# Second attention: the scores from two products with k's high and low parts in one tile, and the rope of k finished on VectorE

## What is computed

```python
q1 = _apply_rope(qp[0], cos, sin); q2 = _apply_rope(qp[1], cos, sin)
...
def block(i):                                     # 128 queries at a time
    qpos = start + jnp.arange(Q_BLOCK)
    mask = kpos[None, :] < ((qpos // CHUNK) + 1)[:, None] * CHUNK
    s1 = jnp.einsum('bhqd,bhkd->bhqk', qb1, k1).astype(jnp.float32) * scale
    s2 = jnp.einsum('bhqd,bhkd->bhqk', qb2, k2).astype(jnp.float32) * scale
    p1 = jax.nn.softmax(jnp.where(mask, s1, -jnp.inf), axis=-1)
    p2 = jax.nn.softmax(jnp.where(mask, s2, -jnp.inf), axis=-1)
    a = (p1 - lam * p2).astype(v.dtype)
    return jnp.einsum('bhqk,bhkd->bhqd', a, v)
```

## Time and profile before

| | |
|---|---|
| median of 3 runs | 1842.66 us (1841.44 to 1843.53) |
| the profiled execution: its own time | 1840.62 us |
| its span, first to last instruction | 1838.8 us |
| PE busy | 1800.9 us, 98% of the span |
| VectorE, ScalarE, GpSimd busy | 733.5, 780.1, 1021.7 us (40%, 42%, 56%) |
| share of PE in the chain that ended last | 90% |
| mean granted clock of PE | 0.994 of full speed |

### The profile page before, as it was taken

One profiled execution on the slowest core, in us unless ns is written; L12 is line 12 of the kernel. 1 busy time (PEld: TensorE's weight loads), 2 busy tenths in 40 slices (PEclk: granted clock), 3 DMA queues, 4 the chain that ended last, 5 costly groups with the idle time before them and its releaser, 6 DMA issues.

```text
span 1838.8 us, 27037 instructions
## 1 busy us (share of the span) xinstructions
PE 1800.9 (98%) x8880; PEld 1500.3 (82%) x8880; DVE 733.5 (40%) x1348; ACT 780.1 (42%) x1612; POOL 1021.7 (56%) x919
## 2 busy tenths in 40 slices
PE   8999999999999999999999999989999999999997
PEld 6879888888887888888888888878887888888886
DVE  7954000001135555453333322456765543333224
ACT  5434323222244555464444422545564644444221
POOL 6856655555462322366666655556554566666651
PEclk9999999999999999999999999999999999999999
DMA  5312333323334544223333233333332233332332
GB/s 150 92 29 86 104 99 95 91 85 105 89 100 100 129 119 114 81 81 103 103 91 103 78 105 91 83 81 86 86 82 56 81 103 95 99 94 86 103 90 96
DMA packets 327250, 171.92 MB, mean 93 GB/s; under 512 B 43458, under 2 KB 316948, under 8 KB 327188
## 3 DMA queue, kind: packets, MB, share of 16 engines
q1 hardware_dynamic: 327172, 171.12, 33.4%
q10 hardware_dynamic: 16, 0.00, 0.0%
HBM read 152.15 MB, written 2.10 MB: 84 GB/s over the span
## 4 chain that ended last, share of the span: by engine, by line
PE 90%; DVE 4%; ACT 2%; POOL 1%; issue 1%; DMA 1%; SPq 0%; DVEq 0%; ACTq 0%; POOLq 0%
PE bank L920 25%; PE bank L921 24%; PE bank L922 24%; PE attended L920 2%; PE attended L922 2%; PE attended L921 2%; PE turned L1317 1%; PE bank L1023 1%; PE bank L1011 1%; PE score L1299 1%; DVE xres L2001 1%; PE score L1301 0%; ACT xres L1510 0%; PE score L1300 0%; DVE small L2271 0%
## 5 line engine op out<-in xcount | busy, mean ns | idle before, releaser
L703 POOL TENSOR_TENSOR WL<-raw,WH 128x512 fp32r<-128x512 f32 (+3 forms) x656 | 776.4, 1206 | 615.2 <-ACT WH L1474 614.5
L920 PE MATMUL bank<-XL,WH 128*128 128x512 f32 x1456 | 579.3, 398 | 7.2 <-DVE XL L2044 3.6
L921 PE MATMUL bank<-XH,WH 128*128 128x512 f32 x1456 | 567.3, 390 | 0.0
L922 PE MATMUL bank<-XH,WL 128*128 128x512 f32 x1456 | 567.1, 389 | 0.0
L1474 ACT ACTIVATE WH<-raw 128x512 fp32r<-128x512 f32 (+3 forms) x656 | 338.3, 565 | 303.9 <-PE bank L922 201.5
L920 PEld LDWEIGHTS bank<-XL,WH 128*128 128x128 f32 x1456 | 274.5, 189 | 62.8 <-DVE XL L2044 4.8
L922 PEld LDWEIGHTS bank<-XH,WL 128*128 128x128 f32 x1456 | 274.4, 188 | 57.8
L921 PEld LDWEIGHTS bank<-XH,WH 128*128 128x128 f32 x1456 | 274.9, 189 | 51.2
L920 PE MATMUL bank<-HL,WH 128*128 128x512 f32 (+1 forms) x528 | 200.5, 380 | 0.0
L921 PE MATMUL bank<-HH,WH 128*128 128x512 f32 (+1 forms) x528 | 200.3, 379 | 0.0
L922 PE MATMUL bank<-HH,WL 128*128 128x512 f32 (+1 forms) x528 | 200.2, 379 | 0.0
(11 more groups left out here) (314 smaller groups left out, 2492.7 us busy)
## 6 DMA issues: line engine op xcount, KB each, us to landing
raw<-in_ffn_w_in SPq DMA_DIRECT2D x88, 512.0 KB, 3.8
raw<-in_w_gate SPq DMA_DIRECT2D x22, 512.0 KB, 3.8
raw<-in_w_up SPq DMA_DIRECT2D x22, 512.0 KB, 3.9
raw<-in_ffn_w_out SPq DMA_DIRECT2D x28, 384.0 KB, 3.4
raw<-in_ffn_w_out SPq DMA_DIRECT2D x28, 320.0 KB, 3.1
raw<-in_a_w_in SPq DMA_DIRECT2D x16, 512.0 KB, 4.1
raw<-in_kv_w SPq DMA_DIRECT2D x32, 256.0 KB, 3.2
raw<-in_w_in SPq DMA_DIRECT2D x12, 512.0 KB, 3.9
```

Source lines behind the costliest of these rows:

```text
L703: pool.tensor_tensor(wl, x, wh, ALU.subtract).then_inc(w_lo, 1)
L920: pe.matmul(out_, wh, xl, start=start, stop=False)
L921: pe.matmul(out_, wh, xh, start=False, stop=False)
L922: return pe.matmul(out_, wl, xh, start=False, stop=stop)
```

## The change

**Tiles.** `KD[:, c, :]` holds for map c the high part of k in this map's own rows and the low part of the same map in the other map's rows. `QD[:, slot, c, :]` holds q's high part in both sets of rows, and `QZ[:, slot, c, :]` q's low part in the own rows and zeros in the others. QD times KD is then high with high plus high with low, and QZ times KD is low with high (with zeros for the rest). So a score has two products with 128 rows. The mask becomes a product of 64 rows and 64 columns between the two: only the upper half of the queries' chunk and the last 64 keys of a block need it. KD is single, and QD and QZ are double; KD and the low part QL lie in the unused halves of PTH and PTL.

**Engines.** The sum of k's rope moves from GpSimd to VectorE: the sine products go first, the cosine product is written back into the PSUM bank, and `tensor_tensor` adds the two. ScalarE makes two high copies each of q (both maps' tiles) and k. k's low parts are made by VectorE, four subtractions of 32 rows (`k_lows`), after slot 10. GpSimd keeps the sum and low part of q, except in the first unit, where VectorE does both. The DMAs are still 8 a unit: 4 carry rows of q within QD, 4 carry QL into QZ.

The diff, cut to what is spoken of (in the lines left out are semaphores, the first unit's order on ScalarE, and the loop count of VectorE, 42 for 40):

```diff
@@ -280,9 +280,10 @@
         dif = ExitStack()
-        QKH = sb("QKH", [P, 2, 2, S], F32R, stack=dif)
-        QKL = sb("QKL", [P, 2, 2, S], F32R, stack=dif)
-        QHZ, QLZ = (x[:, 1, 0:2 * S].rearrange("p (c s) -> p c s", c=2) for x in (PTH, PTL))
+        QD = sb("QD", [P, 2, 2, S], F32R, stack=dif)
+        QZ = sb("QZ", [P, 2, 2, S], F32R, stack=dif)
+        KD = PTH[:, 1, 0:2 * S].rearrange("p (c s) -> p c s", c=2)
+        QL = PTL[:, 1, 0:S]
         rope = sb("rope", [P, 2, S], stack=dif)
@@ -643,15 +646,17 @@
                     sp.wait_ge(zeros_ready, 2)
-                else:
-                    for c in range(2):
-                        sp.wait_ge(s_done[c], 4 * (UNITS + u))
-                slot, lo_count = u % 2, 2 * u + 1
-                for z, x, ready, count in ((QHZ, QKH, qk_hi, 2 * UNITS + lo_count), (QLZ, QKL, qk_lo, lo_count + OPEN)):
-                    sp.wait_ge(ready, count)
-                    for c in range(2):
-                        for r in rows_of_map(c):
-                            sp.dma_start(z[r, c, :].bitcast(F32), x[r, slot, 0, :].bitcast(F32)).then_inc(q_padded, 16)
+                slot = u % 2
+                own_rows, other_rows = [rows_of_map(c) for c in range(2)], [rows_of_map(1 - c) for c in range(2)]
+                sp.wait_ge(q_top, 2 * u + 2)
+                for r, o in zip(own_rows[1], other_rows[1]):
+                    sp.dma_start(QD[o, slot, 1, :].bitcast(F32), QD[r, slot, 1, :].bitcast(F32)).then_inc(q_padded, 16)
+                sp.wait_ge(qk_lo, u + 1 + OPEN)
+                for r, o in zip(own_rows[0], other_rows[0]):
+                    sp.dma_start(QD[o, slot, 0, :].bitcast(F32), QD[r, slot, 0, :].bitcast(F32)).then_inc(q_padded, 16)
+                for c in range(2):
+                    for r in own_rows[c]:
+                        sp.dma_start(QZ[r, slot, c, :].bitcast(F32), QL[r, :].bitcast(F32)).then_inc(q_padded, 16)
@@ -859,19 +864,16 @@
-            for x in (QHZ, QLZ):
-                pool.memset(x.bitcast(F32), 0.0).then_inc(zeros_ready, 1)
-            def rope_sum(iu, j):
-                pool.wait_ge(bank_read[j], iu.times(4, STAGES["qkv2"][1] + j).round(2, 1))
+            def rope_sum(iu):
+                pool.wait_ge(bank_read[0], iu.times(4, STAGES["qkv2"][1]).round(2, 1))
                 pool.tensor_tensor(qk[:, :], qk[:, :], rot_sin[:, :], ALU.add).then_inc(roped, 1)
-            def rope_low(iu, j):
-                pool.wait_ge(qk_hi, iu.times(2, 2 * UNITS + j).n(1))
-                pool.tensor_tensor(QKL[:, iu.slot(2), j, :], qk[:, :], QKH[:, iu.slot(2), j, :].bitcast(F32),
-                                   ALU.subtract).then_inc(qk_lo, 1)
+            def rope_low(iu):
+                pool.wait_ge(q_top, iu.times(2).n(1))
+                pool.wait_ge(q_padded, iu.times(128).n())
+                pool.tensor_tensor(QL[:, :], qk[:, :], QD[:, iu.slot(2), 0, :].bitcast(F32), ALU.subtract).then_inc(qk_lo, 1)
@@ -1296,10 +1294,10 @@
                 pe.wait_ge(ex[c], used.n() + OPEN)
-                pe.matmul(sc[c][:, k], QLZ[:, c, q], QKH[:, slot, 1, k], start=True, stop=False)
-                pe.matmul(sc[c][:, k], QHZ[:, c, q], QKH[:, slot, 1, k], start=False, stop=False)
-                pe.matmul(sc[c][:, k], QHZ[:, c, q], QKL[:, slot, 1, k], start=False, stop=False)
-                pe.matmul(sc[c][:, q], identr[:, :], masks[:, 1, :], start=False, stop=True).then_inc(s_done[c], 1)
+                pe.matmul(sc[c][:, k], QD[:, slot, c, q], KD[:, c, k], start=True, stop=False)
+                pe.matmul(sc[c][0:CHUNK, i * P + CHUNK:(i + 1) * P], identr[0:CHUNK, 0:CHUNK], masks[0:CHUNK, 1, CHUNK:P],
+                          start=False, stop=False)
+                pe.matmul(sc[c][:, k], QZ[:, slot, c, q], KD[:, c, k], start=False, stop=True).then_inc(s_done[c], 1)
@@ -1416,7 +1414,8 @@
                             pe.wait_ge(q_padded, u.times(128).n(128))
-                            pe.wait_ge(qk_lo, u.times(2, 2).n() + OPEN)
+                        if sl < 2:
+                            pe.wait_ge(k_low, u.times(2, sl).n(1))
                         score(sl, u.times(4, first + sl // 2), slot, sl // 2)
@@ -1830,8 +1829,14 @@
-                act.wait_ge(roped, iu.times(2, j + 1).n())
-                act.activation(QKH[:, iu.slot(2), j, :], qk[:, :], ACT.Copy).then_inc(qk_hi, 1)
+                if j or first_unit(iu):
+                    act.wait_ge(bank_read[j], iu.times(4, STAGES["qkv2"][1] + j).round(2, 1))
+                else:
+                    act.wait_ge(roped, iu.n())
+                src = rot_k if j else qk
+                for c in range(2):
+                    to = KD[:, c, :] if j else QD[:, iu.slot(2), c, :]
+                    act.activation(to, src[:, :], ACT.Copy).then_inc(k_top if j else q_top, 1)
@@ -2370,20 +2375,42 @@
                 scale = 1.0 if j else HEAD ** -0.5
+                in_bank = j == 1 or first_unit(iu)
                 dve.wait_ge(item_done, iu.times(4, STAGES["qkv2"][0] + j + 1).n())
-                dve.wait_ge(qk_lo, iu.times(2, j).n() + OPEN)
-                own.did(dve.scalar_tensor_tensor(out=qk[:, :], in0=bank[j][:, :], scalar=scale, in1=rope[:, 0, :],
-                                                 op0=ALU.mult, op1=ALU.mult))
+                if not in_bank:
+                    dve.wait_ge(qk_lo, iu.n() + OPEN)
+                    own.did(dve.scalar_tensor_tensor(out=qk[:, :], in0=bank[j][:, :], scalar=scale, in1=rope[:, 0, :],
+                                                     op0=ALU.mult, op1=ALU.mult))
+                rot = rot_k if j else qk if in_bank else rot_sin
                 for h in range(2):
                     of, to = slice(HEAD * h, HEAD * h + HEAD), slice(HEAD - HEAD * h, P - HEAD * h)
-                    if h:
+                    if h and not in_bank:
                         own.sync()
-                    ins = dve.scalar_tensor_tensor(out=rot_sin[to, :], in0=bank[j][of, :], scalar=scale, in1=rope[of, 1, :],
+                    ins = dve.scalar_tensor_tensor(out=rot[to, :], in0=bank[j][of, :], scalar=scale, in1=rope[of, 1, :],
                                                    op0=ALU.mult, op1=ALU.mult)
-                    if h:
+                    if h and not in_bank:
                         ins.then_inc(bank_read[j], 1)
                     else:
                         own.did(ins)
+                if in_bank:
+                    own.sync()
+                    own.link(dve.scalar_tensor_tensor(out=bank[j][:, :], in0=bank[j][:, :], scalar=scale, in1=rope[:, 0, :],
+                                                      op0=ALU.mult, op1=ALU.mult))
+                    dve.tensor_tensor(rot[:, :], bank[j][:, :], rot[:, :], ALU.add).then_inc(bank_read[j], 1)
+            def first_q_low(iu):
+                dve.wait_ge(q_top, 1)
+                dve.tensor_tensor(QL[:, :], qk[:, :], QD[:, 0, 0, :].bitcast(F32), ALU.subtract).then_inc(qk_lo, 1)
+            def k_lows(iu):
+                for c in range(2):
+                    dve.wait_ge(k_top, iu.times(2, c + 1).n())
+                    for i, (r, o) in enumerate(zip(rows_of_map(c), rows_of_map(1 - c))):
+                        ins = dve.tensor_tensor(KD[o, c, :], rot_k[r, :], KD[r, c, :].bitcast(F32), ALU.subtract)
+                        if i == 1:
+                            ins.then_inc(k_low, 1)
@@ -2401,7 +2428,9 @@
                     rope_products(iu, 0)
+                    first_q_low(iu)
                     rope_products(iu, 1)
+                    k_lows(iu)
                     make_lambda()
@@ -2418,8 +2447,10 @@
                         map_lo(i % 2, au.times(2, first + i // 2), 0, i)
-            weave_units(counted(40), diff_part)
+                if iu is not None:
+                    k_lows(iu)
+            weave_units(counted(42), diff_part)
             head_scaled(Nth(UNITS - 1))
```

More of the change, by code:

```diff
@@ L295, in two_blocks @@
         CC = work[:, 5, :].bitcast(F32R)
+        rot_k = work[:, 5, :]
         gate_z, gate_e, gate_one = (pmap[0:FOX_HEADS, i, :] for i in (1, 2, 3))
@@ L883, in unit_lows @@
                     next_low(iu, 1)
-                    rope_sum(iu, 0)
                     next_low(iu, 2)
-                    rope_low(iu, 0)
-                    rope_sum(iu, 1)
-                    rope_low(iu, 1)
+                    for slot in range(2):
+                        pool.memset(QZ[:, slot].bitcast(F32), 0.0).then_inc(zeros_ready, 1)
                     next_low(iu, 3)
@@ L1843, in diff_part @@
                     rope_hi(iu, 0)
+                    rope_hi(iu, 1)
+                    unit_high("qkv2", iu, 3)
+                    value_out("qkv2", iu)
                     act.wait_ge(lam_c, 1)
                     act.activation(lam_row[1], lam_row[0], ACT.Exp).then_inc(lam_c, 1)
-                    value_out("qkv2", iu)
-                    rope_hi(iu, 1)
-                    unit_high("qkv2", iu, 3)
                     return
```

7 lines of the change are left out of this document (3 added, 4 removed).

## The result

The changed kernel took 1848.15 us (median of 8 runs, 1845.8 to 1849.35), the kernel before 1842.41 (8 runs, 1841.44 to 1843.53): a ratio of 1.0029, interval 1.0019 to 1.0038. It is 5.7 us slower. The forecast was 1832.7, in a range from 1828.5 to 1839.5. The profiled execution took 1848.35, with a span of 1846.6.

What follows compares the result with a forecast made beforehand. PE was taken to bound the kernel (busy 98% of the span). Gains of 1.4 + 6 x (1.5 - 0.2) + 0.75 = 9.95 us took the profiled 1840.62 to 1830.6; with 2.04 for the median, 1832.7, range 1828.5 to 1839.5.

Steps and rivals of the forecast that it cites:

- PE's mask term: PE's score stream: each new, smaller mask costs 0.02 to 0.03 us less, bounds 0.05 more to 0.06 less.
- The fourth rival: PE's scores: small mask tile hinders loads on both sides, 0.05 each, 64 times, 3.2 us; 1835.9 us, chance 0.06.
- the first unit: First unit of the second attention: 0.5 from an earlier start plus 0.9 within it, 1.4 us less.
- All up to there is unchanged: VectorE, from slot 4's row maximum to the start of k's rope at +11.04: nothing changes.
- The second rival: VectorE bounds steady units: q's low part on GpSimd holds slot 8's combination, 1.07 of 1.5 lost; 1838.0 us, chance 0.16.
- The two products: PE's scores: a unit loses two products of each size, 1.29 us less.
- Cosines, sum, low parts: VectorE's new work in a unit: cosine product 0.72 us, sum 0.69, four low parts of k 2.7.
- The 0.2 a unit for a hold on k's low parts: Steady units: GpSimd's next weights hold VectorE's fourth subtraction, so PE waits some 0.2 us for map 1.
- The margin before the product with v: VectorE's low part ends at 14.6, PE arrives at 14.84: margin 0.2 us, so PE still bounds, barely.
- The last unit and what follows: Last unit: PE waits for combined maps; VectorE's chain starts 0.75 us earlier, so the gain is 0.75, not 1.5.
- The first score: First unit's start: PE's first score comes between 0 and 1.75 us earlier; 0.5 taken, as one hold is likely.
- the sum: Whole kernel: first unit, six steady units and last unit together give 9.95, say 10 us less.

Runs made afterwards that it cites:

- before_small: Kernel before, three products kept, with the 64x64 mask between the second and third product; 1856.24 us, ratio 1.0073 to the kernel before.
- half_mid: Changed kernel, its mask in the same place but with 128x128 weights and the last 64 keys as moving columns; 1843.01 us, ratio 1.0004 to the kernel before.
- rows64: Changed kernel with mask weights of 64 rows and 128 columns, in the middle; 1847.87 us in a single run.
- cols64: Changed kernel with mask weights of 128 rows and 64 columns, in the middle; 1842.95 us, ratio 1.0008 to the kernel before.
- experiment 7: both_first, with lambda's sums ahead of q's low part and lambda's row ahead of k's low parts in the first unit; 1830.12 us, ratio 0.9937.
- full_last: Changed kernel with the mask again a full 128x128 product behind the others; 1842.64 us, ratio 1.0003 to the kernel before.
- experiment 5: Also combine_first: full_last, with GpSimd's weights of slot 8 waiting for VectorE's combination of the last two maps; 1833.59 us, ratio 0.9959.
- both_first: full_last with two GpSimd waits: slot 8's weights for VectorE's combination, the next weights for k's low parts; 1832.51 us, ratio 0.9953.

## Why the prediction was wrong

**The step that failed first** is PE's mask term: "I take 0.02 to 0.03 less each", with a bound of "0.05 more each (a small tile that hinders the next load)". It was 0.25 more each, which turned the gain of 1.3 us forecast for a unit into 0.70 lost. I had bounded it by a short product in front of a load that lies beside it. What happens is another thing: the load of a 64-row tile isn't made beside the running product at all, but starts with its own product, 0.27 after the one ahead, and the load of the product behind it starts only with that product too (1271.74). before_small, half_mid, rows64 and cols64 show it. The fourth rival named the right place ("the small mask tile hinders the loads on both sides") with a price of 0.05 a side and 3.2 us in all; measured are 0.37 - 0.11 = 0.26 a mask at 384 keys, and 13.8 us in all in before_small. The range missed for this reason, and the first unit added to it: forecast 1.4 less, measured 1.5 more (3.71 less 2.23).

A row shown before held the warning. Lambda's product has one row, and two of it with one column each take 0.31 us of PE's stream (1210.21 to 1210.52 in before, 1207.34 to 1207.65 in experiment 7) and start 0.20 behind a mask of a score of 128 keys, where 0.11 is usual. Their first load, too, starts with its product (1207.34). I read that row for its time alone, not for its distances.

**A second step fails as soon as the mask is mended.** It is "All up to there is unchanged", said of VectorE from slot 4 to k's rope. In the changed kernel it holds. But with PE's gain the order in time against GpSimd changes, though VectorE's own instructions don't: ScalarE's weights come 0.25 us earlier against VectorE's chain (0.68 ahead of the combination for 0.43). The second rival had the mechanism (a hold at slot 8's combination, 1.07 of 1.5 lost, 1838.0), but with q's low part as the holder and 0.16 as its chance. The runs show the weights of slot 8 as the holder, 1.12 us, and with the hold on k's low parts all of the gain lost (full_last, units of 25.7 for 25.56 before).

The rule of the Trainium skill that the prediction drew on ("SBUF — State Buffer", "Who interferes with whom": two SBUF inputs on VectorE, a read on GpSimd, the later one waits in full) agrees with 1.87 for 0.75 and with what one wait gave back in experiment 5. The forecast had applied it to the four new subtractions only, and the second rival to one old pair, not to each old pair whose distance changes. My row for it was ill read: the operation at 1396.74 has one tile as its input, and what it sat out is the second of the two subtractions (1396.64 to 1397.93), as the first had ended at 1396.69.

**What held.** The two products: 1.29 forecast, 1.27 measured. Cosines, sum, low parts: within 0.1 us. The 0.2 a unit for a hold on k's low parts: 0.3 (combine_first against both_first, 24.6 against 24.29), though the changed kernel has no such hold in its steady units. The margin before the product with v: PE reaches it without a wait in both_first's steady units, as "PE bounds, barely". The last unit and what follows: 0.66 less in both_first for 0.75 forecast, but this stretch scatters by over 1 us between kernels. The first score came 2.2 us earlier counted from the rope, for 0.5 taken and 1.75 as its bound, and lambda's row then took more than that back in the unit, until it was moved. With the full mask and the two waits, the whole was 1838.8 - 1829.1 = 9.7 us of span (8.5 by the medians), where the sum had 10. That it comes so close is in part luck: both_first has neither the 0.2 a unit that the small mask was to save nor the 0.2 that a hold was to cost, and they cancel in the sum; the start and first unit gave 2.05 for 1.4, and scatter ahead of them took 0.63. The price of a product was sound, and so was the rest of PE's stream, with two conditions that the sum left out.

## What to carry to other kernels

Before a product is made smaller, look in the stream of PE and PEld whether a tile of that shape is loaded beside the running product: here a tile with 64 rows of weights cost 0.25 us more each time, and 64 columns or half the moving columns gained nothing. When the bounding engine gets quicker, list every pair of VectorE and GpSimd operations that start close to each other, changed or not, and which of the two moves with the quick engine: a wait on the engine with time to spare can be worth the whole gain. When one cost is mended, look again before the change is judged: a quicker engine can bring out a second one that wasn't there.

## What the runs showed of the hardware that was not expected

- A weight tile of 64 rows (64x64, 64x128) between products of 128 rows is loaded only with its own product (within 3 ns in all 64 masks of after, before_small and rows64, with a median of 0.24 to 0.31 us idle before the load, "issue"); one of 66 rows, of 128 rows, or of 128 rows and 64 columns is loaded beside the product ahead. A mask of 64x128 costs more than one of 64x64: units of 26.68 and 26.25. At the kernel's beginning tiles of 88, 117 and 124 rows are loaded ahead too, 0.07 to 0.23 us before their products, and one of 8 rows only with its own. Whether a tile of 64 rows would load quickly behind another of 64 rows was not tried.
- A difference of 0.25 to 0.3 us in when ScalarE hands weights to GpSimd moves a VectorE operation from 0.75 to 1.87 us, in six units alike.
- A mask product of 128x128 weights costs 0.11 to 0.12 us with what it takes from the product behind it, at 384 and at 512 keys, with 128 moving columns as with 64.
- The granted clock falls to the lower level in the first unit of every kernel here, for 3.4 or for 6.8 us, just after PE's waits at its start.
